# A fused attention and recurrence layer on one core: all keys turned by VectorE and DMA, state updates two units later, ga4 and gb4 ahead of the first projections

## What is computed

```python
h = rms_norm(x, norm_g) * (1 + scale) + shift
qa, ka, va, za, qb, fb, ib, zb = split(h @ w_in)
ya = window_attention(rope(norm(qa)), rope(norm(ka)), va, sinks) * silu(za)     # 8 heads of 64, window 128
k_in, log_f = (1 - lb) * sigmoid(-fb), log(lb + (1 - lb) * sigmoid(fb))
# recurrence, 4 heads of 128: S_new = exp(L_last) * S + (k_in * exp(L_last - L)).T @ ib
#                             o = (qb * exp(L)) @ S + A @ ib
yb = rms_norm(o, o_norm_g) * silu(zb)
g_a, g_b = split(sigmoid(h @ w_merge + b_merge))
y = g_a * (ya @ w_proj_a) + g_b * (yb @ w_proj_b)
out = x + gate * (y @ w_out)
```

## Time and profile before

| | us |
|---|---|
| median of 3 runs | 1563.71 |
| lowest, highest | 1563.18, 1566.8 |
| the profiled execution | 1566.84 |
| its span, first to last instruction | 1564.7 |
| PE busy | 1521.3 (97%) |
| POOL busy | 829.1 (53%) |
| DVE busy | 813.1 (52%) |
| ACT busy | 535.5 (34%) |
| mean granted clock of TensorE, as a share of full speed | 0.993 |

### The profile page before, as it was taken

How to read it: one execution, slowest core, us unless ns; L and a number is a source line. 1 busy time by engine, 2 the same in 40 slices (tenths; PEclk the granted TensorE clock), 3 DMA queues, 4 the chain that set the end, 5 groups by cost and what they waited for, 6 DMA issues and landing times.

```text
span 1564.7 us, 31594 instructions
## 1 busy us (share of the span) xinstructions
PE 1521.3 (97%) x12952; PEld 1236.9 (79%) x12952; DVE 813.1 (52%) x1972; ACT 535.5 (34%) x1111; POOL 829.1 (53%) x1074
## 2 busy tenths in 40 slices
PE   5999999899999999999999999999999999999998
PEld 2777788777888777878879878887888977887887
DVE  5766465234558865531444774642353775742122
ACT  4334323434322532334331452233432352243330
POOL 1525433656863643465774482446786363437671
PEclk9999999999999999999999999999999999999999
DMA  9612213534553321453343231353544231243341
GB/s 347 231 55 83 83 56 95 162 110 161 175 195 104 111 71 57 122 148 108 136 162 136 92 119 43 96 121 123 207 155 148 75 109 56 83 122 111 105 166 59
DMA packets 119048, 191.52 MB, mean 122 GB/s; under 512 B 57199, under 2 KB 74952, under 8 KB 118121
## 3 DMA queue, kind: packets, MB, share of 16 engines
q1 hardware_dynamic: 118904, 189.52, 36.8%
HBM read 169.13 MB, written 18.25 MB: 120 GB/s over the span
## 4 chain that ended last, share of the span: by engine, by line
PE 91%; DVE 4%; SPq 1%; POOL 1%; ACT 1%; issue 1%; DMA 1%; DVEq 0%
PE ps_D L799 54%; PE ps_D L796 25%; PE ps_XCD L861 1%; SPq L522 1%; PE ps_XB L937 1%; PE ps_XA L962 1%; PE ps_XA L973 1%; PE ps_XA L999 1%; PE ps_XB L990 1%; PE ps_XB L989 1%; PE ps_XA L937 1%; POOL w_lo_t L1753 1%; DMA th_t<-in_w_ada 1%; PE ps_XB L973 0%; PE ps_XCD L962 0%
## 5 line engine op out<-in xcount | busy, mean ns | idle before, releaser
L1753 POOL TENSOR_TENSOR w_lo_t<-w_raw,w_hi_t 128x256 fp32r<-128x256 f32 x920 | 684.3, 778 | 593.1 <-ACT w_hi_t L1021 592.6
L799 PE MATMUL ps_D<-h_hi_t,w_hi_t 128*128 128x512 f32 x1024 | 409.1, 400 | 0.0
L799 PE MATMUL ps_D<-h_lo_t,w_hi_t 128*128 128x512 f32 x1024 | 399.4, 390 | 0.0
L799 PE MATMUL ps_D<-h_hi_t,w_lo_t 128*128 128x512 f32 x1024 | 399.3, 390 | 0.0
L1021 ACT ACTIVATE w_hi_t<-w_raw 128x1024 fp32r<-128x1024 f32 x232 | 240.3, 1051 | 123.5 <-PE ps_D L796 61.0
L799 PEld LDWEIGHTS ps_D<-h_hi_t,w_hi_t 128*128 128x128 f32 x1024 | 192.2, 188 | 47.7 <-issue 9.8
L799 PEld LDWEIGHTS ps_D<-h_hi_t,w_lo_t 128*128 128x128 f32 x1024 | 192.2, 188 | 41.4
L799 PEld LDWEIGHTS ps_D<-h_lo_t,w_hi_t 128*128 128x128 f32 x1024 | 192.5, 188 | 37.2
L796 PE MATMUL ps_D<-w_hi_t,h_hi_t 128*128 128x384 f32 (+1 forms) x384 | 141.5, 369 | 1.0 <-DVE yf_t L1387 1.0
L796 PE MATMUL ps_D<-w_lo_t,h_hi_t 128*128 128x384 f32 (+1 forms) x384 | 136.5, 356 | 0.0
L796 PE MATMUL ps_D<-w_hi_t,h_lo_t 128*128 128x384 f32 (+1 forms) x384 | 136.2, 355 | 0.0
(11 more groups left out here) (386 smaller groups left out, 2330.4 us busy)
## 6 DMA issues: line engine op xcount, KB each, us to landing
w_raw<-in_w_blocks SPq DMA_DIRECT2D x232, 512.0 KB, 3.4
xr<-in_x_prompt SPq DMA_DIRECT2D x16, 512.0 KB, 5.4
x_or_AT<-in_x_prompt SPq DMA_DIRECT2D x14, 512.0 KB, 5.2
out_dram<-xr SPq DMA_DIRECT2D x12, 512.0 KB, 2.9
z_o<-kk SPq DMA_DIRECT2D x8, 512.0 KB, 3.1
x_or_AT<-in_x_turned SPq DMA_DIRECT2D x3, 1024.0 KB, 5.4
p_or_hf<-in_x_turned SPq DMA_DIRECT2D x3, 1024.0 KB, 5.4
z_k<-kk SPq DMA_DIRECT2D x4, 512.0 KB, 4.6
```

The lines of the kernel that those rows point to most:

```text
L799: ins = mm(bank[:, :], w[:, s0, k0 + k, :], a[:, k, :], start=go, stop=end)
L1753: ins = g_.tensor_tensor(w_lo[:, c, k:k + 2], w_raw[:, n % NRAW, k:k + 2], f32(w_hi[:, c, k:k + 2]), ALU.subtract)
```

## The change

All keys go the way of the second half (`KEYS_TURNED = (0, 1)`): `KT` on PE and its copy on ACT are gone, `kD` stands twice on VectorE at half 56, and both halves go through `z_k` and come back into `k_turned`. `o` and `st` move by four halves (two units), and onorm, yD, yT and the events of o with them, by two units or a little more. In the units' order ga4 and gb4 come ahead of pa0 (so that pa0 is unit 38 and pb0 unit 39, instead of 36 and 37), and the later gates are regrouped. ga4 and gb4 get slots in `ff`, for which ACT waits until the last state update is done. The events of the keys have the numbers 27 and 27.1 instead of 28 and 28.

```diff
-    out = [(c, j) for j in range(4) for c in ("ga", "gb")]
+    out = [(c, j) for j in range(5) for c in ("ga", "gb")]
     for j in range(8):
-        out += [("pa", j), ("pb", j)] + ([("ga", j + 2), ("gb", j + 2)] if 1 < j < 6 else [])
+        out += [("pa", j), ("pb", j)] + [(c, {2: 5, 3: 6, 5: 7}[j]) for c in ("ga", "gb") if j in (2, 3, 5)]
     return out
...
-KEYS_TURNED = (1,)
-O_AT, ON_AT, YD_AT, YT_AT = (57, 59, 61, 63), (60, 64), (65, 66, 69, 70), (66, 67, 70, 71)
-KS_AT, KL_AT, OS_AT, OL_AT = (28, 28), (28, 28), (30, 32), (31, 32)
+KEYS_TURNED = (0, 1)
+O_AT, ON_AT, YD_AT, YT_AT = (61, 63, 65, 67), (64, 68), (71, 72, 75, 75), (72, 73, 76, 77)
+KS_AT, KL_AT, OS_AT, OL_AT = (27, 27), (27.1, 27.1), (32, 34), (32.1, 34.1)
...
-            put(it, (40, 41, 46, 47)[_n], 1, "xst", _t)
+            put(it, (42, 43, 46, 47)[_n], 1, "xst", _t)
...
-            _u = (43, 52)[_r]
+            _u = (44, 52)[_r]
...
-TH.update({(c, j): (4, 6, 0, 2, 0, 2, 0, 2)[j] + (c == "gb") for j in range(8) for c in ("ga", "gb")})
+TH.update({(c, j): (4, 6, 0, 2, 8, 0, 2, 0)[j] + (c == "gb") for j in range(8) for c in ("ga", "gb")})
...
+            if n >= 8:
+                return ff[:, n - 8, :]
...
-                    later.setdefault(b0 + 43, []).append(("x01", it, 0))
+                    later.setdefault(b0 + 44, []).append(("x01", it, 0))
...
-            later.setdefault(40, []).append(("ckv", 0, 0))
+            later.setdefault(41, []).append(("ckv", 0, 0))
...
-                elif task == "KT":
-                    s.wait_ge("lvl", 8 * it + 8)
-                    for h in range(HB):
-                        ins = tr(bank[:, P * h:P * h + P], kk[:, h, P * a:P * a + P], ident[:, :])
...
                 elif task == "st":
-                    if a < 2:
-                        s.freed(it, "KT", a)
-                    else:
-                        s.wait_ge("kt_in1", 64 * (it + 1))
+                    s.wait_ge(f"kt_in{a // 2}", 64 * (it + 1))
                     for h in range(HB):
-                        left = kst[:, h, :] if a < 2 else k_turned[:, 1, h, a % 2, :]
-                        ins = mm(bank[:, P * h:P * h + P], left, ibtok[:, a, P * h:P * h + P],
+                        ins = mm(bank[:, P * h:P * h + P], k_turned[:, a // 2, h, a % 2, :], ibtok[:, a, P * h:P * h + P],
                                  start=True, stop=True)
...
+                    if (kind, j) == ("ga", 4):
+                        s.freed(it, "st", 3)
...
-                elif task == "KT":
-                    s.full(*key)
-                    if a:
-                        s.full(it, "st", a - 1)
-                    s.free(fn(kst, bank[:, :].rearrange("p (h n) -> p h n", h=HB), ACT.Copy), *key)
```

## The result

| | before | changed |
|---|---|---|
| median, us | 1565.26 | 1581.18 |
| lowest, highest | 1563.18, 1567.02 | 1579.56, 1582.57 |
| the profiled execution, its span | 1566.84, 1564.7 | 1580.98, 1578.9 |

The account below looks back on a forecast made before the run. PE, busy 97% of the span, was taken as the bound. +5.1 + 2.0 - 3.5 - 1.4 + 2.7 = +4.9 us gave 1571.7 for the profiled execution and a median of 1568.6 us, range 1560.5 to 1574.

Parts of the forecast that it names:

- The wait at pb0: First unit of the second projection: PE's wait for POOL grows by one low half, 1.28 us, in four passes; +5.1 us.
- nothing in either order lets POOL start earlier: At pb0: the added wait can't be less unless POOL starts its split earlier; ends +4.8 and +5.4 us.
- Clock in pass 1: Behind pb0's longer wait in pass 1, PE's clock falls as in the other three passes; +2.0 us, ends 0 and 2.8.
- Transposes: Eight groups of four key transposes leave PE's queue, 0.44 us each; -3.5 us.
- The factor of 19: Skill's figure for a plain DMA transposing by strides against the transposing path; the forecast saw no such factor in the landings.
- the third rival: Keys late for PE at 1.6 times the transfer time, +6.9 on the sum, 1575.5 us; chance 0.16 with other late transfers.
- The third o: Pass 0: PE's wait for ACT goes, since the column sum now comes ahead of onorm; -1.4 us.
- The load behind the keys: Pass 0: block 29's load queues behind two key writes on SP, so PE's sample burst waits; +2.7 us, ends 0 and 4.2.
- I take no clock loss: At pass 0's burst: no lower clock behind the wait, as the wait of some 2 us in pass 1 had none.
- The keys: Keys feeding st0 land in time, with margins of 4.3 us in pass 0 and 3.2 in the others; nothing.
- the first conclusion of the prediction: The change is worth what leaves PE's queue, plus or minus waits at pb0 and two places of pass 0.
- the rivals: Not slower, 1563.9 us (0.20); faster, 1558.8 (0.14); late keys, 1575.5 (0.16 with other late transfers).

Follow-up runs that it names:

- e6: The changed kernel with yb's products and roundings of quarter 1 ahead of ga4's drain and split, those of quarters 2 and 3 ahead of gb4's; 1556.54 us.
- e10: The kernel before with yb's products and roundings of quarters 0 and 1 half a unit earlier, quarter 3's rounding ahead of gb3's drain and split; 1548.91 us.
- e13: The changed kernel with 244 waits on a long full semaphore at PE's start, moving later PE instructions by 122 places; 1578.04 us.
- e12: e8 with the first half's keys turned by PE and copied by ACT again; 1551.03 us.
- e8: The changed kernel with keys at event 28 behind block 29's load, row scales one unit earlier, and e6's earlier yb products and roundings; 1545.47 us.
- e5: The changed kernel with VectorE's row scales (rstd) put one unit earlier, at 49 instead of 50; 1575.31 us.
- e1: The changed kernel run again with no edit; 1583.29 us.
- e11: e8 with 122 waits added at PE's start, which became 61 event instructions, so the shift was 61 places; 1541.65 us.
- e9: The kernel before run again with no edit; 1565.04 us.
- e7: The changed kernel with keys at event 28 and the first half's keys turned by PE and copied by ACT again; 1579.42 us.
- e14: e8 with 244 waits at PE's start, moving later PE instructions by 122 places; 1545.91 us.

## Why the forecast was right in sign and wrong in size

- **The wait at pb0**, +5.1: measured 16.5 - 11.6 = +4.9, by the chain that was forecast. What the working said beside it, that nothing in either order lets POOL start earlier, is true, and missed that the low halves need not stand behind that split at all (e6, e10).
- **Clock in pass 1**, +2.0: 0.50 over 3.4 us, 1.7. The size was right. It is not certain, though: in e13 the clock held behind the same wait (3.23).
- **Transposes**, -3.5: e12 against e8 gives 4.9 us in the merges, 5.6 in the medians. The term was too small: 0.5 us for a group by the merges of passes 1 to 3, and a wait for the copy in pass 0. The Trainium skill (VectorE: DVE Perf Modes, Rules for kernel authors) says of a 128x128 transpose: "Use TensorE if PSUM dest is OK; xbar DMA otherwise". That weighs the transpose alone; in this kernel, where PE's time is the time, VectorE's way was the cheaper one by those 4.9 us. The factor of 19 that the prediction names stands in the Trainium skill (VectorE: DVE Perf Modes, The three transpose paths) with the condition that the innermost destination stride is large. Whether these reads meet it no run shows; they landed in 3.3 us, and the third rival was worked out for 1.6 times, not for 19.
- **The third o**, -1.4: the wait went. The working then followed the column sum to ACT only. In pass 0 a later one stands behind `rstd`, and PE waits 1.43 us for it.
- **The load behind the keys**, +2.7: 3.3, by the mechanism forecast. The step that failed is "I take no clock loss": 0.57 over 6.8 us, 2.9. It was read off the one wait of 2 us that had none, though the wait taken (2.7) was nearer to the 3.2 of the three that had. Behind the same wait in e13 the clock held, so this loss is not there in every execution.
- **The keys**, nothing: no wait for k_turned in any pass; the reads landed in 3.3 us on the mean. Rival 3 did not happen.
- **Missing: the row scales**, +4.2 (e5). The step that failed is the first conclusion of the prediction, that the change is worth what it takes from PE's queue, "plus or minus what it does to the waits at pb0 and at two places of pass 0": only places that the diff moves were costed. `rstd`, `bc` and `sT` keep their numbers, while the units under these numbers got shorter.
- **Missing: the stages that nothing was moved in**, +5.4. The sum took them as unchanged, by the same step. 48 matmuls fewer on PE shift the later instructions, and so where an edge of its program falls in the scores (e13, the same work with its instructions moved, is 8.2 us shorter in them): one more wait of 1.1 to 1.7 us in pass 2, shorter ones behind it, and in this execution lower clock behind pass 1's; e1, without that clock, lost 3.4 us in these stages. Without counting instructions no row of the kernel before would have told this.

From the forecast's 1571.7 for the profiled execution to 1580.98 it is 9.3: +4.2 (row scales), +5.4 (the rest stages), +2.9 and +0.6 (burst), -1.4 (transposes, by e12's 4.9), -0.2 and -0.3 (pb0 and its clock), -1.5 (a start that was quicker in this execution) are +9.7, which leaves 0.4 the other way. None of the rivals describes it. The chance for slower was 0.48, and the range left nothing for tasks not looked at.

What the two halves of the change are worth where nothing else waits: the keys on VectorE -5.6 us by the medians and -4.8 by the traces (e12 to e8); the new order, with yb ahead in both, +2.1 by the medians and +0.6 by the traces (e10 to e12), with ratios whose intervals overlap, so that only its parts are clear: by the table it saves 2.6 us in the merges of pass 0 (the third o's wait, and the 1.03 left in e10) and loses 2.8 in the rest stage ahead of pass 3's merges, where an edge falls into the scores. Most of what the changed kernel lost is places of small tasks, which e8 mends: 1545.47, 20 us under the kernel before; e11 gives 1541.65.

## What to carry to other kernels

When units are reordered under a table of numbered tasks, cost the tasks that keep their number too: for each one that PE waits for, add up the PE time between it and its consumer, before and after. When a wait ends with a chain on a helper engine, ask what in the chain need not stand ahead of it; that was worth 16 us here (e10), as much as the change cost. And before a loss in an untouched stage is explained by the change, compare the places of its waits in the engine's instruction order, and move the instructions by a padding that does no work.

## What the runs showed of the hardware

**Edges of the program.** Numbering PE's instructions (weight loads, matmuls, events), every 'issue' wait of 0.25 us or more inside the two kinds of short-matmul bursts (task `dg`, L919 or L921 or L923, and task `level`, L937 or L939 or L941), 59 in the 16 profiles, stands where the number leaves 192 or 193 when divided by 256. A dg burst of passes 1 to 3 is 192 instructions, in 1.05 us where nothing disturbs it. How far into it the edge falls, and the wait there:

| kernels | pass 1 | pass 2 | pass 3 |
|---|---|---|---|
| before, e9, e10 | 170: 1.32 to 1.55 us | 74: none | 120: 0.35, none, none |
| changed, e1 to e6, e8 | 186: 1.52 to 1.88 | 138: 1.14 to 1.70 | 201 (behind it): 0.31 to 0.79 at the next long matmuls in six of eight |
| e7, e12 | 171: 1.00, 1.60 | 106: 0.21, 0.16 | 152: 1.62, 1.39 |
| e11 | 125: 0.34 | 77: none | 140: 1.43 |
| e13, e14 | 64: none | 16: none | 79: none |

Up to 80 there is nothing, from 138 on a wait of 1 us or more. But the depth in the burst is not the cause. In pass 0 the burst is longer, an edge falls 217 instructions into it in all kernels without a padding, and nothing waits:

```profile
185.35 1.30 PE L919 MATMUL ps_XA<-qq,kk 128*32 128x32 f32 x128
```

What decides is when the program itself arrives, and the traces show that. The page of each kernel has a DMA queue that carries instructions (packets, MB, share; here the changed kernel's):

```profile
q8 instruction: 102, 1.67, 0.4%
```

These are 102 transfers of 16384 bytes, and PE's program has 102 edges, in every one of the 16 profiles. With both numbered in order, PE never passed edge n less than 1.20 us after the end of transfer n - 1 (1616 pairs), and transfer n often ended after edge n was passed. Behind the 63 waits of 0.3 us or more at edges PE went on 1.21 to 1.56 us after the end of that transfer. In pass 2 of the changed kernel the edge before was passed at 956.98, the transfer ran from 957.82 to 959.08, and PE went on at 960.29. So the waits are waits for instructions. In passes 1 to 3 eighty more short matmuls (task `PV`, 160 instructions) stand directly ahead of dg; with the edge more than 96 instructions into the burst, all 256 since the last edge are short ones and run in 1.7 to 2.0 us, mostly too fast for the next transfer. In pass 0 long matmuls stand among them and they take 5.5 us.

The Trainium skill (Runtime: NRT & Kernel Launch, Instruction fetch mechanics) says that the program comes in blocks of 256 instructions, each fetched while the one before runs, and that this is mostly hidden. The 256 and the transfers agree with it; hidden it is not where a whole block is short matmuls.

Two other 'issue' waits are of another kind. One of 0.62 to 1.68 us stands ahead of o0 of pass 1 in all 16 profiles, at remainders that go with the kernel (226, 34, 2, 31, 92), and one of 0.36 to 0.39 in fifteen at a small task of the samples in pass 1 (L903, L905 or L907), at an edge only in e11, where the transfer had ended 29.8 us before. Their cause stays open.

**The clock behind a wait.** Over all 16 profiles, and behind the start, PE's clock fell from 2.4 GHz to 1.2 behind 37 of 40 waits of 3.2 us or more, behind two of five of 2.0 to 2.1, and behind four of 55 of 1.2 to 1.9 (all four in the scores). The three exceptions stand at places where others fell: 3.55 us at pb0 of pass 0 in e9, and 3.23 at pb0 of pass 1 and 3.38 at the burst in e13,

```profile
259.60:266.40 6.80, 6.77 (x42) 5.17 (x43) 0.00 (x0) 3.29 (x4) 3.83 (x6) 1.00 0.98 173
```

where the changed kernel had 0.57 behind 3.32. So a forecast can price it (1.6 to 3 us behind a wait over 3 us, in most executions), but one profile doesn't tell a place that has it from one that hasn't.

**Small operations beside POOL.** In the timeline of `rstd` above, VectorE's first operations of 4 columns took 0.65 to 0.67 us each (the very first 0.35) and the later ones 0.16 to 0.17. What changed between them is POOL, whose split ended at 1140.19 (the first short one starts at 1140.24):

```profile
1134.59 5.60 POOL L1744 TENSOR_TENSOR w_lo_t<-w_raw,w_hi_t 128x256 fp32r<-128x256 f32 x8 [2.62 <-ACT w_hi_t L1015]
...
1139.55 0.65 DVE L1242 TENSOR_TENSOR sm<-sm 128x4 f32<-128x4 f32 x1
1140.24 0.17 DVE L1243 TENSOR_SCALAR sm<-sm 128x4 f32<-128x4 f32 x1
```

The first ones follow each other every 0.70 us, and one of POOL's eight instructions lasts as long (5.60 / 8): one small operation for each of them. The kernel before shows it in both directions in one `rstd` of pass 2, between a low half that ends at 1123.17 and a split that starts at 1123.95:

```profile
1121.98 1.21 DVE L1251 TENSOR_TENSOR sm<-sm 128x4 f32<-128x4 f32 x1
1123.23 0.17 DVE L1252 TENSOR_SCALAR sm<-sm 128x4 f32<-128x4 f32 x1
...
1124.03 0.69 DVE L1252 TENSOR_SCALAR sm<-sm 128x4 f32<-128x4 f32 x1
```

That `rstd` lasted 10.3 us, and no matmul waited for it, since unit 50 and 51 took longer there. So a split beside it is what made `rstd` last 6.0 us in the changed kernel; this is read from two traces, no run tested it.
